# Key and value products moved into the opening stage of a two-layer diffusion backbone on one Trainium2 core

## What is computed

```python
# every layer l: six vectors from the condition, and the same six for the context
sh1, sc1, g1, sh2, sc2, g2 = split(silu(c) @ mod_w[l] + mod_b[l], 6)
csh1, csc1, ... = split(silu(c_ctx) @ mod_w[0] + mod_b[0], 6)
# layer 0: attention beside a short gated convolution
pl = (rms_norm(x, g) * (1 + sc1) + sh1) @ ev_w_in            # 2048 -> 4608
pc = (rms_norm(ctx, g) * (1 + csc1) + csh1) @ ev_w_in[:, 1024:1536]   # keys and values
mix = concat(attention(q(pl), [k(pl), k(pc)], [v(pl), v(pc)]), short_conv(pl))
x = x + g1 * (mix @ ev_w_out)
x = x + g2 * (relu(modulate(x) @ w1) ** 2 @ w2)
# layer 1: Hyena: three projections, a long convolution by FFT with filters
h = sin(freq * (sin(freq * (feats @ f_w1 + f_b1)) @ f_w2 + f_b2)) @ f_w3   # 256 x 4096
filt = h * (exp(-t * abs(f_decay)) + 0.05)
x = x + g1 * (hyena(modulate(x), rfft(filt)) @ od_w_out);  x = x + g2 * ffn(...)
return rms_norm(x, final_g)
```

## Time and profile before

| | |
|---|---|
| median of 3 runs | 2467.64 us (2464.17 to 2469.01) |
| the profiled execution | 2467.65 us, its span 2465.9 us |
| mean granted TensorE clock | 0.972 |
| PE / PEld / DVE / ACT busy | 96% / 84% / 74% / 41% of the span |
| first 151 us (until the key/value unit) | PE busy 118 us at a granted clock of 0.76, DMA share 0.93 |
| bytes | 613.8 MB, 249 GB/s over the span |
| chain that ended last, by engine | PE 86%, DVE 6%, DMA 3%, ACT 2%, issue 1% |

### The profile page before, as it was taken

How to read it: one execution, slowest core, us unless ns; L and a number is a source line. 1 busy time by engine, 2 the same in 40 slices (tenths; PEclk the granted TensorE clock), 3 DMA queues, 4 the chain that set the end, 5 groups by cost and what they waited for, 6 DMA issues and landing times.

```text
span 2465.9 us, 37957 instructions
## 1 busy us (share of the span) xinstructions
PE 2372.1 (96%) x14656; PEld 2073.9 (84%) x14656; DVE 1823.9 (74%) x2439; ACT 1015.1 (41%) x963; POOL 0.2 (0%) x4
## 2 busy tenths in 40 slices
PE   6899799998999999999989999999899999999997
PEld 2369478997888888888889989999788888888887
DVE  3557769988888888888888777875878655665565
ACT  4432334434444444444443223233444444444444
POOL 0000000000000000000000000000000000000000
PEclk7789899998999999999999999999999999999999
DMA  9897178996888888888875566556677555555552
GB/s 355 279 327 284 51 267 326 344 339 242 303 292 312 321 299 302 298 320 316 294 260 183 208 225 220 197 196 211 216 283 267 185 190 203 187 178 194 193 189 102
DMA packets 266042, 613.82 MB, mean 249 GB/s; under 512 B 12208, under 2 KB 12336, under 8 KB 265456
## 3 DMA queue, kind: packets, MB, share of 16 engines
q1 hardware_dynamic: 260992, 602.08, 68.6%
...
## 4 chain that ended last, share of the span: by engine, by line
PE 86%; DVE 6%; DMA 3%; ACT 2%; issue 1%; SPq 0%; DVEq 0%; ACTq 0%
PE acc L578 20%; PE aux L578 20%; PE acc L521 17%; PE acc L604 11%; PE aux L604 10%; PE aux L521 2%; PE aux L656 1%; DMA w_raw<-mod_first 1%; ACT w_hi L1401 1%; PE aux L829 1%; PE aux L850 1%; DMA w_raw<-od_w_in 1%; DMA scr<-k_freq 1%; PE aux L518 1%; DVE w_lo L884 1%
## 5 line engine op out<-in xcount | busy, mean ns | idle before, releaser
L884 DVE TENSOR_TENSOR w_lo<-w_raw,w_hi 128x2048 fp32r<-128x2048 f32 x372 | 849.6, 2290 | 260.1 <-ACT w_hi L1401 244.8
L1401 ACT ACTIVATE w_hi<-w_raw 128x2048 fp32r<-128x2048 f32 x372 | 710.1, 1912 | 625.1 <-PE acc L521 278.1
L578 PE MATMUL acc<-act_a,w_hi 128*128 128x512 f32 x1216 | 295.4, 396 | 6.7 <-issue 4.5
L578 PE MATMUL aux<-act_a,w_hi 128*128 128x512 f32 x1216 | 290.1, 391 | 0.0
L578 PEld LDWEIGHTS acc<-act_a,w_hi 128*128 128x128 f32 x1216 | 226.9, 191 | 53.5 <-issue 5.8
L521 PE MATMUL acc<-act_a,w_hi 128*128 128x256 f32 x1920 | 261.7, 287 | 6.1 <-DVE summed L924 3.6
L578 PEld LDWEIGHTS aux<-act_a,w_hi 128*128 128x128 f32 x1216 | 223.4, 188 | 43.3
L521 PEld LDWEIGHTS acc<-act_a,w_hi 128*128 128x128 f32 x1920 | 247.6, 194 | 9.4 <-issue 4.5
L578 PE MATMUL acc<-act_b,w_hi 128*128 128x512 f32 x1024 | 244.3, 391 | 0.0
L892 DVE SCALAR_TENSOR_TENSOR m_raw<-m_raw,wide 128x1024 f32<-128x1024 f32 x180 | 217.7, 1218 | 5.0 <-DMA m_raw<-mod_rest 4.7
L578 PEld LDWEIGHTS acc<-act_b,w_hi 128*128 128x128 f32 x1024 | 188.2, 188 | 36.4
...
## 6 DMA issues: line engine op xcount, KB each, us to landing
w_raw<-ffn_w SPq DMA_DIRECT2D x256, 1024.0 KB, 7.0
...
w_raw<-od_w_in SPq DMA_DIRECT2D x48, 1024.0 KB, 8.1
w_raw<-ev_w_in SPq DMA_DIRECT2D x36, 1024.0 KB, 9.2
w_raw<-mod_first SPq DMA_DIRECT2D x32, 1024.0 KB, 9.6
w_raw<-ev_w_out SPq DMA_DIRECT2D x16, 1024.0 KB, 10.0
w_raw<-od_w_out SPq DMA_DIRECT2D x16, 1024.0 KB, 5.1
```

Of the source, the lines that this page charges most:

```text
L578: return pe.matmul(banks[:, ft, :], w_hi[:, kg % 2, kc * 512 + ft * P:kc * 512 + ft * P + P], rhs[:, k, :], start=(k == 0), stop=False)
L884: TT(w_lo[:, kg % 2, :], w_raw[:, kg, :], w_hi[:, kg % 2, :].bitcast(F32), ALU.subtract)\
L1401: return act.activation(out_, in_, func, **kw)
```

## The change

It has five parts.

1. **Layout.** Every weight matrix is stored quarter by quarter (`quarters` on the host), so that a load is 128 rows of 8 KB instead of 512 runs of 2 KB. The bytes are the same. It holds for all 404 loads of `w_raw`.
2. **Decay.** The 2 MB load of the decay, repeated for 128 partitions, becomes a load of one row of 16 KB; TensorE spreads it (`spread_decay`, eight products), and ScalarE takes the absolute value out of PSUM (`take_decay`). `f_w3` and the transform table are loaded ahead of the first block.
3. **Keys and values.** The quarters of their weights are loaded among blocks 4 to 7 (`PIECES`), in whichever slot comes next, and TensorE takes each of their four quarters between rows of the blocks (`keys_values`), both results in one bank of `aux`. All filter and spectrum work is done before the first.
4. **Norms and silu.** Both input norms are finished at once, and the silu row is spread as the last thing before the fourth quarter, into `acc`.
5. **Modulation units.** With no key/value body left, units 0 and 1 run beside the queries, and units 2 and 3, 16 tiles, inside attention: five between the head rotations, eleven in the softmax steps from the sixth on.

The diff, cut to its core. First the constants, the loads and SP's order:

```diff
-MU_ATTN = 3
+PIECES = []
+for _u in range(START):
+    PIECES += [(_u, _kg) for _kg in range(4)]
+    if 3 <= _u <= 6:
+        PIECES.append((None, _u - 3))
+SEQ = {p: i for i, p in enumerate(PIECES)}
...
+MU_ATTN = 2
...
+            sp.dma_start(decay_row, decay_in).then_inc(decay_landed, 16)
+            for i in range(2):
+                sp.dma_start(fw3[i], fw3_in[:, i, :].rearrange("p (j c) -> p j c", j=4)).then_inc(w3_landed, 16)
+            sp.dma_start(fwd_first, fwd_in).then_inc(fwd_landed, 16)
...
+            def used_up(i):
+
+                u, kg = PIECES[i]
+                if u is None:
+                    sp.wait_ge(lo_done, kg + 1)
+                elif kg == 3:
+                    sp.wait_ge(row_full, u + 1)
                 else:
-                    sp.wait_ge(raw_used, u * 3 + (kg - 2))
+                    sp.wait_ge(raw_used, u * 3 + (kg + 1))
...
-                    sp.dma_start(w_raw[:, kg, :].rearrange("p (c n) -> p c n", c=4),
-                                 w[ds(row + kg * 512, 512), ds(col, 512)].rearrange("(c p) n -> p c n", p=P))\
-                        .then_inc(landed[kg], 16)
+                    sp.dma_start(w_raw[:, kg, :], w[ds(row + kg * across * P, P), :]).then_inc(landed[kg], 16)
...
+            for i, (u, kg) in enumerate(PIECES):
+                if i >= 4:
+                    used_up(i - 4)
+                if u is None:
+                    row = ATTN_W // 4 + kg * 9 * P
+                    sp.dma_start(w_raw[:, i % 4, :], ev_w_in[row:row + P, :]).then_inc(landed[i % 4], 16)
+                else:
+                    row = (kg * 8 + START_COLS[u]) * P
+                    sp.dma_start(w_raw[:, i % 4, :], mod_first[row:row + P, :]).then_inc(landed[i % 4], 16)
+                if (u, kg) == (0, 3):
+                    sp.dma_start(x[:, :, :], x_in).then_inc(x_landed, 16)
+                elif (u, kg) == (1, 3):
+                    sp.dma_start(ctx_raw, ctx_in).then_inc(ctx_landed, 16)
+            unit(U_Q, ev_w_in, 0, 9, mods(0), first=True, slots=EARLY)
+            unit(U_Q + 1, ev_w_in, P, 9, mods(1), mods(0), slots=EARLY)
```

TensorE:

```diff
+            def spread_silu():
+                for i in range(4):
+                    pe.wait_ge(mc_ready, START - 1 if i < 3 else START)
+                    for kc in range(4):
+                        k = 4 * i + kc
+                        mm = pe.matmul(acc[i][:, kc * P:kc * P + P], silu[:, 0, k:k + 1].to_broadcast([P, P]), ident,
+                                       start=True, stop=True)
+                    mm.then_inc(silu_full, 1)
...
+            def spread_decay(i):
+                for j in range(4):
+                    if i:
+                        pe.wait_ge(decay_made, j + 1)
+                    pe.matmul(aux[j][:, :], ones[0:1, :], decay_row[:, 4 * i + j, :], start=True, stop=True)\
+                        .then_inc(decay_full, 1)
...
+            spread_decay(0)
...
+            def keys_values(kg, between=()):
+
+
+                def products(ft, kc, part, a):
+                    k = 4 * kg + kc
+                    w = (w_hi, w_lo)[part][:, kg % 2, kc * 512 + ft * P:kc * 512 + ft * P + P]
+                    for i, rhs in enumerate((act_a, act_b)):
+                        mm = pe.matmul(aux[ft][:, i * T:i * T + T], w, rhs[:, k, a:a + T],
+                                       start=(k == 0 and part == 0 and a == 0 and i == 0), stop=(k == 15 and part == 1 and i == 1))
+                    return mm
...
+                pe.wait_ge(hi_done, kg + 1)
+                steps = list(between)
+                if kg == 3:
+                    for kc in range(4):
+                        pe.wait_ge(normed, 2 * (4 * kg + kc + 1))
+                        for ft in range(4):
+                            for a in (0, T):
+                                mm = products(ft, kc, 0, a)
+                else:
+                    pe.wait_ge(normed, 8 * kg + 8)
+                    for ft in range(4):
+                        for kc in range(4):
+                            for a in (0, T):
+                                mm = products(ft, kc, 0, a)
+                        if ft < 3 and steps:
+                            steps.pop(0)()
+                mm.then_inc(hi_used, 1)
+                pe.wait_ge(lo_done, kg + 1)
+                for ft in range(4):
+                    for kc in range(4):
+                        mm = products(ft, kc, 1, 0)
+                    if kg == 3:
+                        mm.then_inc(psum_full, 1)
+                if kg < 3:
+                    mm.then_inc(ws_free, 1)
+                for step in steps:
+                    step()
...
+            spread_decay(1)
+            pe.wait_ge(silu_ready, 1)
+            mod_rows(0, 0)
+            mod_rows(0, 1)
...
             filters(0, 0)
             filters(0, 1)
+            mod_rows(0, 2)
+            mod_rows(0, 3)
...
+            spectrum(0, (0, 1))
+            mod_turn(0)
+            spectrum(0, (2, 3))
+            mod_rows(1, 0)
+            mod_rows(1, 1)
+            filters(1, 0)
+            filters(1, 1)
+            mod_rows(1, 2)
+            mod_rows(1, 3)
+            spectrum(1, (0, 1))
+            mod_rows(2, 0)
+            mod_turn(1)
+            spectrum(1, (2, 3))
+            mod_rows(2, 1)
+            filters(2, 0)
+            filters(2, 1)
+            mod_rows(2, 2)
+            pe.wait_ge(mc_ready, 1)
+            norm_sums(0, acc[2], 16, sq_sum[:, :])
+            norm_sums(1, acc[2], 18, ctx_sum)
+            mod_rows(2, 3)
+            spectrum(2, (0, 1))
+            mod_rows(3, 0)
+            norm_spread(0, acc[2][:, T:2 * T], sq_sum[:, :])
+            pe.wait_ge(mc_ready, 2)
+            norm_spread(1, acc[3][:, T:2 * T], ctx_sum)
+            spectrum(2, (2, 3))
+            mod_rows(3, 1)
+            filters(3, 0)
+            filters(3, 1)
+            mod_turn(2)
+            mod_rows(3, 2)
+            mod_rows(3, 3)
+            mod_rows(4, 0)
+            spectrum(3, (0, 1))
+            mod_turn(3)
+            mod_rows(4, 1)
+            spectrum(3, (2, 3))
+            mod_rows(4, 2)
+            mod_rows(4, 3)
             pe.wait_ge(kout_ready, 16)
-            gemm(U_KV, act_a, (normed, 0, 2), with_ctx=True, first=True)
-            with pe.Fori(0, 2) as m:
-                gemm(m + U_Q, act_a)
+            keys_values(0, [rows_of(5, 0), lambda: mod_turn(4), rows_of(5, 1), rows_of(5, 2), rows_of(5, 3)])
+            keys_values(1, [lambda: mod_turn(5), rows_of(6, 0), rows_of(6, 1), rows_of(6, 2), rows_of(6, 3)])
+            keys_values(2, [lambda: mod_turn(6), rows_of(7, 0), rows_of(7, 1), rows_of(7, 2), rows_of(7, 3),
+                            lambda: mod_turn(7)])
+            spread_silu()
+            keys_values(3)
+            pe.wait_ge(silu_wide, 4)
+            gemm(U_Q, act_a, first=True)
+            gemm(U_Q + 1, act_a)
```

VectorE, the opening stage and attention:

```diff
+            def input_norms():
+
+                root(4, acc[2][:, 16:20], 2, ms_full, var_ready, root_ready, D_MODEL)
+                for n, dst in enumerate((sq_sum[:, :], ctx_sum)):
+                    for tt in range(2):
+                        ins = TS(dst[:, tt * P:tt * P + P], ident, stat[:, 3, 2 * n + tt:2 * n + tt + 1], None, ALU.mult)
+                    ins.then_inc(diag_ready, 1)
+
+            def both(j):
+                windowed(j, 0)
+                windowed(j, 1)
+
+            both(0)
+            squares_in(0, sq_sum[:, :])
             first_modulation(0)
-            norm(0, acc[2][:, 16:18])
-            dve.wait_ge(bc_full, 1)
-            squares_in(1)
-            windowed(1, 0)
+            both(1)
+            squares_in(1, ctx_sum)
             first_modulation(1)
-            windowed(1, 1)
+            both(2)
+            input_norms()
             first_gains(0)
-            norm(1, acc[3][:, 16:18])
             modulate(0, ctx_items(0), 2)
             first_modulation(2)
...
+            both(3)
+            lo(0, 0, True)
+            first_modulation(3)
+            first_gains(1)
+            lo(0, 1, True)
+            modulate(8, ctx_items(1), 2)
+            first_modulation(4)
+            first_modulation(5)
+            first_gains(2)
+            modulate(16, ctx_items(2), 2)
+            lo(0, 2)
+            first_modulation(6)
+            lo(0, 3)
+            first_modulation(7)
             first_gains(3)
-            lo(0, 0, True)
             modulate(24, ctx_items(3), 2)
-            lo(0, 1, True)
...
             dve.wait_ge(silu_wide, 4)
-            body(U_KV, keys_values, mod=0, slots=EARLY)
+            lo(1, 0)
+            for ft in range(4):
+                dve.wait_ge(psum_full, ft + 1)
+                dve.tensor_copy((kT if ft < 2 else vT)[:, ft % 2, :], aux[ft][:, :]).then_inc(psum_free, 1)
...
-                body(m + U_Q, lambda: queries(m), mod=m + 1, slots=EARLY)
...
+            def attention_tile(i):
+                mod_tiles([(MU_ATTN + i // 8, i % 8)], NARROW)
...
```

(51 more changed lines are left out.)

217 lines of the change are left out of this document (65 added, 152 removed).

## The result

The changed kernel takes 2484.92 us (median of 4 runs, 2481.22 to 2491.4) against 2467.41 before (4 runs): ratio 1.0070, 95% interval 1.0058 to 1.0082, so 17.5 us **slower**. The forecast was 2465.3, range 2454 to 2475. The profiled execution of the changed kernel is its slowest run, 2491.4 us with a span of 2489.6; it is 23.7 us longer than the profiled one of before, and 6.2 of that is not in the medians.

A forecast was written before the change was run, and what follows sets the result against it. The opening was taken as bound by a chain over three engines, not the bytes, and the key/value unit by TensorE. Opening -11, attention +8.7, layout 0 sum to -2.3 from about 2467.65: 2465.3 us, range 2454 to 2475.

The forecast's parts named there:

- the gain of 11 in the opening: Start of the kernel up to the query products: these start at 188 us instead of 199.1.
- Start: Opening up to the first spectrum: it starts at 26 us instead of 41.2, with decay products of 0.99 us each.
- Rounds: Opening, filters, product, spectrum and copies three times: second, third and fourth spectrum at 47, 68 and about 101.6 us.
- filters to 87: Opening, last round: filters done at 87 us, ScalarE having waited for a key/value quarter whose slot falls free at 73.
- From the fourth spectrum to the key/value products: Opening: spectrum, turn and three quarters of rows take 14.3 us, last copies 1.6 more, first key/value quarter at 117.5.
- Key/value quarters: Stage before the queries: products 46.1, rows 12.5, turns 4.2, silu spread 6.3, sum 69.1 us, plus a 0.5 wait.
- lower bound of 2: Opening: if rounds keep the 28.5 us of the last two before, queries start at 197, 2 us earlier.
- Attention: Eight more tiles on VectorE cost 5.9 between head rotations, 2.3 in softmax steps, 0.5 at the end: +8.7 us, 7 to 10.
- Layout: All 404 weight loads in longer runs: worth nothing; bounds -0.9 and +4 us per Hyena block.
- The third rival: Hyena blocks: second spectrum load held back, at 10.5 instead of 8.05 us costing +10, total 2475; chance 0.13.
- signs of being wrong: Fourth spectrum before 95 or after 108 us, attention's pair staying at 4.8 us, or the second spectrum load over 9.
- The second rival: Opening and attention: rounds do not close up, attention pays in full; gain 2, cost 9, total 2474.6; chance 0.14.

The follow-up runs named there:

- warm_up: The changed kernel with four products on zeroes put ahead of and among TensorE's first products, before the decay products; ratio 1.0056 to the kernel before.
- code_pad: The changed kernel with nine more long-met wait instructions on VectorE near its start, putting its first MLP loop back at its old place; ratio 1.0055 to the kernel before.

## Why the forecast was wrong

The direction: the gain of 11 in the opening did not come, and two losses that the sum had at nothing came, the layout's in Hyena and one in the first MLP.

1. *Start, wrong.* Forecast 26, measured 33.0. The term that failed is "8 products of 512 columns, each 0.99 us", from the filter step's row at full clock; they took 1.79. I had named 1.98 as the other end, and the earlier trace rows speak for it: the silu spread, at the same place in the program, took 6.26 us there, and as many columns of a spectrum half 3.68; its own products take 3.82 at 183 us in the changed kernel. warm_up shows for the first four that the clock, not the row, is the cause.
2. *Rounds, wrong in the fourth.* Forecast 47, 68 and 101.6, measured 52.1, 74.1 and 114.2: the first two late by the start and no more (19.1 and 22.0 us apart for 21 and 21), the fourth by 6.5 more. The step "filters to 87" failed: the key/value quarter landed at 86.6, the filters began at 90.2, at half clock, and ended at 97. I had the wait, but put the slot's release at 73, 5 us behind the third spectrum's start; it came at 81.9, 7.8 behind it, since that spectrum's first half, after a wait of 3.56, took 6.73 us instead of 3.7. And I left out what the gap ahead of the filters does to the clock. The chain copy, modulate, filter product was as I had walked it: 10.0 us idle, as forecast.
3. *From the fourth spectrum to the key/value products* 15.2 us, forecast 15.9: right.
4. *Key/value quarters* 69.1 us, forecast 69.1 and 0.5: right, in part by luck. The silu spread took 2.4 less there, and waits of TensorE, 1.2 and 0.6 us for weights and 0.7 for a row copy, took it back.
5. *Sum of the opening*: 0.4 instead of 11, below even the lower bound of 2, which held the start at 26. Of the 10.6 us that are missing the start makes 7.0 and the fourth round 6.5; the other steps, with the 0.9 left for small waits, gave 3 back.
6. *Attention* +10.1, forecast +8.7, 7 to 10: right in mechanism, slightly small. Up to the first maximum 42.1 us instead of 35.8 (+6.3, forecast 5.9), the softmax steps +2.5 (forecast 2.3), their end +1.3 (0.5). A pair of steps with two tiles takes 5.4 us, forecast 5.6.
7. *Layout*, taken as nothing: wrong. It costs 10.0 us in Hyena in the profiled execution, 5.2 alone, and 4.5 to 10.2 over the kernels that share that code. The third rival was the right one, with 10 us and a chance of 0.13; I had let two stores of a spectrum in the opening (6.2 and 6.4 us) speak against it; stores with another fill of the other queue were no measure of this load. Longer pieces in SP's queue hold the load back (8.1 to about 10 us), and longer pieces of its own free it (10.0 to 7.8 us), as I had drawn it from the rule of the Trainium skill that I cited (DMA: Bandwidth & Descriptors, Queues, rings and completion order); that the engines switch at packets is not itself seen in a trace. The price was more than the delay: 2.0 us of load, then 1.7 us of half clock in the inverse.
8. *Not in the forecast at all*: 3.2 us in the first MLP, by a stall where VectorE's loop jumps back. code_pad shows that the loop's place in the code sets it; that it is the loading of code rests on the packets of the instruction queue and on the section of the Trainium skill cited there.

Two of the signs of being wrong came: the fourth spectrum after 108, and the load over 9. The second rival's time for the opening and attention (gain 2, cost 9) nearly came too, but not its mechanism: from the first spectrum to the fourth it is 81.1 us instead of 95.9 before, so the rounds did close up, by less than forecast.

By the sum of stages -0.2 + 10.1 + 0.2 + 3.2 + 10.0 + 0.4 = 23.7 in the profiled execution. What the medians lack of it is not located, since no profile of the changed kernel at 2485 was taken; the likeliest place is Hyena, where kernels with the same code took up to 5.5 us less than this execution.
